# Two-block network on one core: memory columns earlier in the first mixer, a decay factor one stage ahead, cross-attention values together, leading tile in two token pieces

## What is computed

```python
def second_block(...):
    h = x
    for l in range(DEPTH):                      # DEPTH = 2
        u = rms_norm(h, g_mix_pre[l])
        if l % 2 == 0:
            u = mlstm_rglru_mixer(u, ...)       # 4 mLSTM heads of 128, 4 RG-LRU blocks of 128
        else:
            u = sliding_window_sink_attention(u, ...)
        h = h + rms_norm(u, g_mix_post[l])
        u = memory_cross_attention(rms_norm(h, g_x_pre[l]), mem, g_mem[l], w_xq[l], w_xkv[l], w_xo[l])
        h = h + rms_norm(u, g_x_post[l])
        u = squared_relu_mlp(rms_norm(h, g_ff_pre[l]), w_ff1[l], w_ff2[l])
        h = h + rms_norm(u, g_ff_post[l])
    return h
```

## Time and profile before

| | us |
|---|---|
| median of 3 runs (lowest, highest) | 3482.1 (3479.43, 3483.46) |
| the profiled execution | 3482.05 |
| its span, first to last instruction | 3480.3 |
| PE busy in it | 3372.4 |
| DVE, ACT, POOL busy | 1779.9, 1336.1, 62.4 |

### The profile page before, as it was taken

How to read it: one execution, slowest core, us unless ns; L and a number is a source line. 1 busy time by engine, 2 the same in 40 slices (tenths; PEclk the granted TensorE clock), 3 DMA queues, 4 the chain that set the end, 5 groups by cost and what they waited for, 6 DMA issues and landing times.

```text
span 3480.3 us, 38047 instructions
## 1 busy us (share of the span) xinstructions
PE 3372.4 (97%) x15558; PEld 2757.9 (79%) x15558; DVE 1779.9 (51%) x2697; ACT 1336.1 (38%) x2111; POOL 62.4 (2%) x65
## 2 busy tenths in 40 slices
PE   9999989999999999899999999999999989999999
PEld 7888767888878887678888778777888778778887
DVE  4333785433463337854334865546444665655443
ACT  3222555322242226543322544334332565434332
POOL 0000000000000000000000000000000000000000
PEclk9999999999999999999999999999999999999999
DMA  5332311333323333114333233222333313213332
GB/s 162 97 96 86 79 49 55 109 97 97 97 85 97 97 91 79 49 53 117 100 94 97 68 102 98 85 60 77 102 96 99 79 55 91 74 52 111 97 97 69
DMA packets 604285, 304.09 MB, mean 87 GB/s; under 512 B 43600, under 2 KB 601808, under 8 KB 603984
## 3 DMA queue, kind: packets, MB, share of 16 engines
q1 hardware_dynamic: 604112, 301.66, 30.2%
HBM read 299.52 MB, written 2.10 MB: 87 GB/s over the span
## 4 chain that ended last, share of the span: by engine, by line
PE 77%; DVE 12%; ACT 7%; issue 2%; DMA 1%; SPq 0%; DVEq 0%; ACTq 0%
PE ps L1681 24%; PE ps L1682 24%; PE ps L1689 24%; DVE wl L2080 2%; ACT wh L1863 1%; DVE tmp L2089 1%; DVE Y L2251 1%; ACT XH L1907 1%; PE ps L1848 1%; PE ps L1832 1%; PE ps L1750 1%; DVE XL L2160 1%; DVE XR L2174 1%; PE ps L1735 1%; ACT tmp L1934 1%
## 5 line engine op out<-in xcount | busy, mean ns | idle before, releaser
L1681 PE MATMUL ps<-XH,wh 128*128 128x512 f32 x2600 | 1045.2, 402 | 26.3 <-DVE wl L2080 12.2
L1689 PE MATMUL ps<-XL,wh 128*128 128x512 f32 (+1 forms) x2856 | 1063.3, 382 | 0.0
L1682 PE MATMUL ps<-XH,wl 128*128 128x512 f32 x2600 | 1018.1, 392 | 0.0
L2080 DVE TENSOR_TENSOR wl<-raw,wh 128x1024 fp32r<-128x1024 f32 (+1 forms) x565 | 680.4, 1209 | 534.8 <-ACT wh L1863 534.5
L1863 ACT ACTIVATE wh<-raw 128x1024 fp32r<-128x1024 f32 (+1 forms) x565 | 584.9, 1040 | 552.6 <-PE ps L1689 486.8
L1689 PEld LDWEIGHTS ps<-XL,wh 128*128 128x128 f32 x2856 | 540.6, 189 | 105.1 <-DVE XL L2084 0.3
L1681 PEld LDWEIGHTS ps<-XH,wh 128*128 128x128 f32 x2600 | 492.0, 189 | 145.4 <-issue 21.8
L1682 PEld LDWEIGHTS ps<-XH,wl 128*128 128x128 f32 x2600 | 491.9, 189 | 100.5 <-issue 3.1
L1681 PE MATMUL ps<-HHa,wh 128*128 128x512 f32 x1088 | 428.8, 394 | 15.2 <-DVE HLa L2084 11.5
L1682 PE MATMUL ps<-HHa,wl 128*128 128x512 f32 x1088 | 423.8, 390 | 0.0
L1689 PE MATMUL ps<-HLa,wh 128*128 128x512 f32 x1088 | 408.0, 389 | 0.0
(11 more groups left out here) (331 smaller groups left out, 3092.3 us busy)
## 6 DMA issues: line engine op xcount, KB each, us to landing
raw<-in_ffn_w_gu SPq DMA_DIRECT2D x176, 512.0 KB, 3.8
raw<-in_w_ff SPq DMA_DIRECT2D x128, 512.0 KB, 4.0
raw<-in_ffn_w_down SPq DMA_DIRECT2D x64, 512.0 KB, 3.6
raw<-in_w_xkv SPq DMA_DIRECT2D x32, 512.0 KB, 3.9
raw<-in_ev_w_in SPq DMA_DIRECT2D x25, 512.0 KB, 3.9
raw<-in_ffn_w_down SPq DMA_DIRECT2D x32, 384.0 KB, 3.2
raw<-in_w_in SPq DMA_DIRECT2D x24, 512.0 KB, 3.9
raw<-in_w_out SPq DMA_DIRECT2D x64, 128.0 KB, 2.7
```

What stands on the lines that cost most here:

```text
L1681: e.matmul(bank[:, 0:n], t.wh[u % SPL][:, k, :], h, start=first, stop=False)
L1682: e.matmul(bank[:, 0:n], t.wl[u % SPL][:, k, :], h, start=False, stop=False)
L1689: m = e.matmul(bank[:, 0:n], t.wh[u % SPL][:, k, :], l, start=False, stop=last)
L2080: self.e.tensor_tensor(wl, raw, f32(wh), ALU.subtract).then_inc(self.s["lo"], self.tag("lo", f"lo.{i}"))
```

## The change

1. **Pieces.** Behind `post_norm`, and behind `block_norm` for ln2 and ln3 where a feed-forward follows at once (`soon`), tile 0 is made in two pieces of 256 tokens, and the six `p_first` matmuls of the three leading units become twelve of half the width. In `soon` norms PE waits for `XH` alone, not for `XR` too. `p_bn_scale`, `p_post_scale` and `p_post_add` get a slice of tokens.
2. **Memory in the first mixer.** It is loaded into `HX`, a name for the room of the first four `HHa` tiles, right after `pre_scale`, ahead of the two small loads of gate matrices. `normed` is taken three pieces at a time after each head's o column, `parts` all together after the last o column, and each job n below 16 carries unit n.
3. **Decay.** `p_lambda` goes from `mixer2` into `memory_rms`, which runs in the second chunk of the feed-forward before.
4. **Cross.** For head 3 the yields between the four turns and between the two values go.
5. **Window attention.** Two pieces of `normed` after each of the queries 4 to 7, not eight after query 4.

```diff
...
         self.Y = sb("Y", [P, KD, T])
+        with nc.sbuf_tensor("HX", [P, 4, T], F32) as HX:
+            self.HX = HX
...
             hi = xs[k][-1]
-            self.p_first(us, k, n, n_k == 0, h, hi)
+            for i, (c, key) in enumerate(parts if parts and n_k == 0 else [(slice(0, n), hi)]):
+                self.p_first(us, k, c, n_k == 0 and i == 0, h, key)
...
         pend = None
+        soon = which != "ln1" and nxt is None
...
                 g, b = self.t.vec(f"{which}_g", l * KD + m), self.t.vec(f"{which}_b", l * KD + m)
-                self.p_bn_scale(k, m, q, sb, rb, (st, f, self.xr[m]), rt)
-                self.p_bn_affine(k, m, q, g, b, nxt is None, self.x_free[m])
+                cut = HALVES if m == 0 and soon else (ALL,)
+                self.p_bn_scale(k, m, q, sb, rb, (st, f, self.xr[m]), rt, cut)
+                self.p_bn_affine(k, m, q, g, b, nxt is None, self.x_free[m], cut)
+                if len(cut) > 1:
+                    self.parts = (cut[0], f"{k}.h0"), (cut[1], f"{k}.h")
...
                 self.xr[j] = f"{kj}.lo"
-                self.xs[j] = (self.t.XH[:, j, :], self.t.XL[:, j, :], f"{kj}.lo", (f"{kj}.h", f"{kj}.x"))
+                self.xs[j] = (self.t.XH[:, j, :], self.t.XL[:, j, :], f"{kj}.lo",
+                              f"{kj}.h" if soon else (f"{kj}.h", f"{kj}.x"))
...
-    def scaled_split(self, m, name, l):
+    def scaled_split(self, m, name, l, early=None):
...
         g = self.t.vec(name, l * KD + m)
-        self.p_scaled_hi(k, m, g, (self.xr[m], self.x_free[m]))
+        if early:
+            self.p_scaled_hi(f"{k}.hi0", m, g, (early, self.x_free[m]), HALVES[0])
+            self.p_scaled_hi(f"{k}.hi", m, g, self.xr[m], HALVES[1])
+            self.parts = (HALVES[0], f"{k}.hi0"), (HALVES[1], f"{k}.hi")
+        else:
+            self.p_scaled_hi(f"{k}.hi", m, g, (self.xr[m], self.x_free[m]))
...
         for m in range(KD + 1):
+            early = None
...
                 k = self.uid("post")
-                self.p_post_scale(f"{k}.y", m, rb, self.t.vec(name, l * KD + m), (rt, self.ys[m]))
+                if m == 0:
+                    early = f"{k}.x0"
+                    self.p_post_scale(f"{k}.y0", m, rb, self.t.vec(name, l * KD + m), (rt, self.ys[m]), HALVES[0])
+                    self.p_post_add(early, m, (f"{k}.y0", self.xr[m]), HALVES[0])
+                self.p_post_scale(f"{k}.y", m, rb, self.t.vec(name, l * KD + m), (rt, self.ys[m]),
+                                  ALL if m else HALVES[1])
...
             if m < KD:
-                self.p_post_add(f"{k}.x", m, (f"{k}.y", self.xr[m]))
+                self.p_post_add(f"{k}.x", m, (f"{k}.y", self.xr[m]), ALL if m else HALVES[1])
                 self.xr[m] = f"{k}.x"
-                pend = self.scaled_split(m, *nxt)
+                pend = self.scaled_split(m, *nxt, early)
...
+        mem = Memory(self, 0, t.HX[:, :, :], [self.hid_free[s] for s in range(4)])
+        mem_normed = mem.normed()
...
-        s1, f = self.tmp.take()
-        z, zf = self.tmp.take()
-        zz, zzf = self.tmp.take()
-        self.p_lambda(f"{kk}.lam", s1, z, zz, (f, zf, zzf))
-        self.tmp.give(z, f"{kk}.lam")
-        self.tmp.give(zz, f"{kk}.lam")
-        self.tmp.give(s1, f"{kk}.lam")
...
             self.psum.give(ob, to)
+            for _ in range(3):
+                next(mem_normed, None)
+            if h == 3:
+                self.x_used(ot)
+                for _ in mem.parts():
+                    pass
+                for s in range(4):
+                    self.hid_free[s] = [self.hid_free[s], mem.raw_done]
...
             qkvo.append((tq, tk, tv, k))
-        self.x_used(ot)
...
         self.tmp.give(rx, lru_state[3])
-        mem = Memory(self, 0, t.XM[:, 4:8, :], self.x_free)
...
-        def memory_parts():
-            yield from mem.normed()
-            yield from mem.parts()
...
-        prep = memory_parts()
...
-        MEM2 = {n: (n - 5,) if n < 17 else (2 * n - 22, 2 * n - 21) for n in range(5, 19)}
...
                 r = late.pop()()
-            for _ in range(4):
-                next(prep, None)
-            for i in MEM2.get(n, ()):
-                mem.unit(i)
+            if n < 16:
+                mem.unit(n)
...
+    def decay(self):
...
+        self.lam = self.uid("lambda")
+        tmps = [self.tmp.take() for _ in range(3)]
+        self.p_lambda(self.lam, *[x[0] for x in tmps], [x[1] for x in tmps])
+        for x, _ in tmps:
+            self.tmp.give(x, self.lam)
...
             query(i)
-            if i == 4:
-                for _ in mem.normed():
-                    pass
+            for _ in range(2):
+                next(mem_normed, None)
...
                         self.d["memT"].rearrange("(k p) t -> p k t", p=P), self.y_free)
+        self.decay()
...
             for b in range(NB):
-                yield
+                if h < 3 or b == 0:
+                    yield
...
             for j in range(2):
-                yield
-                yield
+                if h < 3 or j == 0:
+                    yield
+                    yield
...
                 hold.wait_ge(*at(f))
-            e.matmul(bank[:, 0:n], t.wh[u % SPL][:, k, :], h, start=first, stop=False)
-            e.matmul(bank[:, 0:n], t.wl[u % SPL][:, k, :], h, start=False, stop=False)
+            e.matmul(bank[:, c], t.wh[u % SPL][:, k, :], h[:, c], start=first, stop=False, skip_group_check=True)
+            e.matmul(bank[:, c], t.wl[u % SPL][:, k, :], h[:, c], start=False, stop=False, skip_group_check=True)
...
-    def p_bn_affine(self, k, m, q, g, b, halves, x_free):
+    def p_bn_affine(self, k, m, q, g, b, halves, x_free, cut):
         e, hold, at, t = self.e, self.hold, self.at, self.t
-        hold.wait_ge(*at(f"{k}.q"))
...
                 hold.wait_ge(*at(f))
-            e.activation(t.XH[:, m, :], q[:, :], ACT.Identity, bias=b, scale=g).then_inc(
+            for s in cut[:-1]:
+                hold.wait_ge(*at(f"{k}.q0"))
+                e.activation(t.XH[:, m, s], q[:, s], ACT.Identity, bias=b, scale=g).then_inc(
+                    self.s["act"], self.tag("act", f"{k}.h0"))
+        hold.wait_ge(*at(f"{k}.q"))
+        if halves:
+            s = cut[-1]
+            e.activation(t.XH[:, m, s], q[:, s], ACT.Identity, bias=b, scale=g).then_inc(
...
```

More of the change, by code:

```diff
@@ L319, in __init__ @@
         self.filler = [None, 1, 0, 1]
+        self.parts = None
         self.xr = [f"x.{k}" for k in range(KD)]
@@ L400, in drain, with project_group @@
         self.filler[0] = None
-    def project_group(self, cols, xs, k0=0, order=None):
+    def project_group(self, cols, xs, k0=0, order=None, parts=None):
         nk = len(xs)
@@ L429, in start @@
         def start(order=None, lead=LEAD):
-            got.extend(self.project_group(todo[:lead], xs, 0, order))
+            got.extend(self.project_group(todo[:lead], xs, 0, order, self.parts))
+            self.parts = None
         def ahead():
@@ L1688, in p_last @@
         for u, bank, free in us:
-            m = e.matmul(bank[:, 0:n], t.wh[u % SPL][:, k, :], l, start=False, stop=last)
+            m = e.matmul(bank[:, 0:n], t.wh[u % SPL][:, k, :], l, start=False, stop=last, skip_group_check=True)
             if last:
@@ L1902, in p_bn_affine, with p_scaled_hi @@
             self.s["act"], self.tag("act", f"{k}.x"))
-    def p_scaled_hi(self, k, m, g, after):
+    def p_scaled_hi(self, k, m, g, after, s=ALL):
         for f in flat(after):
             self.hold.wait_ge(*self.at(f))
-        self.e.activation(self.t.XH[:, m, :], self.t.XR[:, m, :], ACT.Copy, scale=g).then_inc(
-            self.s["act"], self.tag("act", f"{k}.hi"))
+        self.e.activation(self.t.XH[:, m, s], self.t.XR[:, m, s], ACT.Copy, scale=g).then_inc(
+            self.s["act"], self.tag("act", k))
     def p_silu(self, key, q, gb, after):
@@ L2143, in p_bn_scale @@
         self.hold.wait_ge(*self.at(rt))
-        self.e.tensor_tensor(q[:, :], q[:, :], rb[:, :], ALU.mult).then_inc(
+        for s in cut[:-1]:
+            self.e.tensor_tensor(q[:, s], q[:, s], rb[:, s], ALU.mult).then_inc(
+                self.s["dve"], self.tag("dve", f"{k}.q0"))
+        s = cut[-1]
+        self.e.tensor_tensor(q[:, s], q[:, s], rb[:, s], ALU.mult).then_inc(
             self.s["dve"], self.tag("dve", f"{k}.q"))
```

21 lines of the change are left out of this document (12 added, 9 removed).

## The result

The changed kernel takes 3463.4 us (median of 4 runs, 3462.0 to 3463.7) against 3481.5 (median of 4, 3479.4 to 3483.5): a ratio of 0.9950, 95% interval 0.9938 to 0.9962. It is faster by 18 us where 25.5 were forecast: 7 us above the point, inside the range by 1.6. The profiled execution took 3463.37, 18.7 less than the one of before.

What follows compares the result with a forecast made beforehand. PE bounds the kernel, busy 3372.4 of 3480.3 us, leaving at most 108 idle plus half-clock stretches. Terms -3.7 - 9.3 - 6.4 - 4.5 - 2.1 + 0.5 = -25.5 take 3482.05 to 3456.5 us; range 3450 to 3465.

Steps and rivals of the forecast that it cites:

- the signs that it named: Expected in the profile after: no 4.98 convolution wait, loop 84 us at clock 1.00, one 0.7 cross wait, changed norm waits.
- rival 1: Loop less cleanly filled, gives 5; weaker clock, first head 2, window attention 2.4; total 3464.6 us, chance 0.15.
- Loop, -9.3: mLSTM loop: memory units from job 0 keep PE fed, so 83.5 us against 93.4, with 0.6 kept back.
- Cross, -6.4: Cross output projections: turns and values together end late splits and cold starts, -3.2 us each, two of them.
- Block norms, -2.1: Three block norms: pieces start PE earlier, but the low half still needs XR, so -0.7 us each.
- post norms, +0.5: Five post norms: PE starts earlier but waits at tile 1 for the DVE and ACT chain, +0.1 us each.
- The doubled matmuls, 0.17 for twelve halves: Behind the norms: twelve half-width matmuls cost 0.17 us more than six whole, within the same wait; the skill's figure gives 0.
- Decay and first head, -3.7: First LRU head: start 3.2 us earlier, clock gains 1.7, three memory pieces before the next convolution cost 1.2.
- after a short idle the clock should hold, which gives 3.98 - 2.26 = 1.7: First LRU head: two matmul pairs run at the second head's 1.13 us each instead of 2.07 and 1.91.
- Window attention, -4.5: Six fewer pieces ahead of the norm PE waits 3.5 us for save 2.4; recovered clock gives 2.1.
- The other pieces go where DVE is half busy: Window attention: the six memory pieces moved from behind query 4 were taken to cost nothing in their new places.
- the 2.1 for the clock: Window attention: of up to 3.1 us lost at clock 0.53 behind the wait, 2.1 come back.

Runs made afterwards that it cites:

- whole post tiles: Changed kernel with the leading tile behind the post norms scaled, added and split whole again, block norms keeping their two pieces; 3461.8 us.
- matrices first: Changed kernel with the two small gate-matrix loads issued ahead of the 1 MB memory load instead of behind it; 3460.5 us.
- units late: Changed kernel with memory still prepared early, but its units issued in the loop steps of the kernel before; 3471.6 us.
- decay in the mixer: As matrices first, but with the 24 small decay operations back in the mixer ahead of the first x product; 3465.1 us.

## Why the prediction was right, and where its sum was off

Right in sign and in range, and the signs that it named came: a short wait for a DMA in place of the 4.98, a loop of 83.7 us at clock 1.00, one wait of 0.7 in each cross attention, and waits for `XH` of tile 1 and for `XL` behind the norms. The terms for the loop, cross and the norms held; two terms came out 6.1 short, two stages outside the sum lost 3.8, and the first block's clock gave 3.1 back. That the time is near rival 1's 3464.6 is chance in the main: its 4.3 in the loop did not occur, only its weaker clock at the first head and in the window attention did.

- *Loop, -9.3:* measured -9.22. The first four jobs with units run full at clock 1.00. Undoing the units gave back 7.8; the other 1.4 were not tried by themselves.
- *Cross, -6.4:* -3.19 and -3.18, one wait of 0.7 each, none for HLa; +3.26 and +3.23 when undone.
- *Block norms, -2.1:* -1.9, held back by the low half as reckoned (at each of the three PE now waits 0.2 for `XL`); *post norms, +0.5:* +0.1 at each of the five, read inside the norm.
- *The doubled matmuls, 0.17 for twelve halves:* in the timeline behind a post norm the twelve take 1.58 us (2207.26 to 2208.84), six whole ones at 0.23 take 1.38, so 0.2. The Trainium skill's rule (TensorE: Matmul & The Clock Gate, "LDWEIGHTS (loading the stationary operand)"), which gave 0, fits less well.
- *Decay and first head, -3.7:* the step that failed is "after a short idle the clock should hold, which gives 3.98 - 2.26 = 1.7". The start (3.04 earlier for 3.2 forecast, the DMA as the new wait) and the pieces (+1.4 at the second head for +1.2) were right. But the clock was at half behind 1.94 us of idle, and behind the second head's longer wait it fell again, 1.6 more. Swapping two loads removed both, and the wait for the DMA is what the two groups of kernels differ in; whether it falls in one run of a kernel is not settled by the wait alone (five of seven).
- *Window attention, -4.5:* two steps failed. "The other pieces go where DVE is half busy" took a mean for a queue: each pair stood ahead of a norm that PE waits for and cost its 0.8 again. And the 2.1 for the clock were not kept, since the attention's own waits behind the last query took up what came early.
- *Not in the sum at all:* the out-projection behind the loop, +2.3, because the units taken from the loop's end had kept PE fed there (shown by two kernels with units back at the end; some 1.6 of it is the clock, which fell in six of eight kernels without them). And +1.5 ahead of the second cross queries, a wait of 1.9 for the norm's row where before 0.4. The row's scale stands on ACT behind the rounding of the last query column's weights, and that waits for their load. ACT before, and then in the changed kernel:

```profile
3006.22 1.06 ACT L1863 ACTIVATE wh<-raw 128x1024 fp32r<-128x1024 f32 x1 [4.86 <-DMA raw<-in_w_xq]
```

```profile
2990.73 1.06 ACT L1889 ACTIVATE wh<-raw 128x1024 fp32r<-128x1024 f32 x1 [6.43 <-DMA raw<-in_w_xq]
```

In all fourteen traces PE's spread of the row follows 2.46 us behind the start of this rounding. The load landed 3.9 us after its issue before and 5.4 in the changed kernel; in the others, which have no edit in this stage but for the whole post tiles of some, 4.3 to 5.5. With 4.3 to 4.6 the stage was 0.9 to 1.1 shorter than in the changed kernel (seven, the four with whole post tiles among them), with 5.1 to 5.5 within 0.2 (three) or, with a stretch at half the clock behind the wait, 1.5 longer (two). So I take it in the main for no part of the change; why one load lands sooner than another stays open, and the 3.9 lies below all the others.

## What to carry to other kernels

When work is moved into an idle place, look for what it covered where it stood: the loop's end lost 2.3 us of the 9.2 that its start won. Half-busy is no place: a small operation was free where its own engine waited in its queue for another one, and cost its full time ahead of what the critical engine waited for. Put a large early load behind the small ones that are needed first, and judge edits of a few us by stages in the trace, as untouched code alone moved the total by 3 us and more.

## What the runs showed of the hardware

- The clock did not follow the length of the wait ahead: with 3.37 us of idle at the second LRU head it stayed at 1.00 (matrices first), with 2.77 there it was at half from 1981.0 on (changed kernel), with 2.11 at the first head it held and with 1.94 it fell, and with 0.86 before the last spread of the loop at half behind it (0.54 over 3.7 us) in the changed kernel, while the same wait in the kernel before had full clock around it. What decides between such cases no run here separates.
- A stretch at half the clock costs what PE's work in it makes of it. The kernels with 6.8 us of such stretches in the window attention in place of 17.1 (units late, decay in the mixer) were 1.3 us shorter there, not 5, for most of the 17.1 lay where PE waits for DVE and ACT; one of 3.4 us in a full stretch cost 1.6.
- 256 KB issued behind 1 MB on SP's queue landed after 7.0 us, and after 4.5 ahead of it, while the 1 MB took 7.1 instead of 6.7.
